# A sink column written by VectorE in place of a one-column product on TensorE, in the banded attention of block 1

## What is computed

```python
def swa_sink_attention(q, k, v, sinks):
    ...
    s = jnp.einsum('bnqhgd,bnkhd->bnhgqk', qb, kk).astype(jnp.float32) * (d ** -0.5)
    ...
    s = jnp.where(mask[None, :, None, None], s, -jnp.inf)
    sink = sinks.astype(jnp.float32).reshape(HKV, G)[None, None, :, :, None, None]
    m = jnp.maximum(jnp.max(s, axis=-1, keepdims=True), sink)
    pexp = jnp.exp(s - m)
    probs = pexp / (jnp.sum(pexp, axis=-1, keepdims=True) + jnp.exp(sink - m))
    o = jnp.einsum('bnhgqk,bnkhd->bnqhgd', probs.astype(v.dtype), vv)
```

## Time and profile before

| | |
|---|---|
| median of 3 runs | 3224.66 us |
| lowest and highest | 3222.48 and 3225.09 us |
| span of the profiled execution | 3222.8 us |
| TensorE busy | 3112.3 us, 97% of the span |
| VectorE busy | 1793.2 us, 56% |
| ScalarE busy | 1251.4 us, 39% |
| mean granted TensorE clock | 0.973 of full speed |

### The profile page before, as it was taken

How to read it: one execution, slowest core, us unless ns; L and a number is a source line. 1 busy time by engine, 2 the same in 40 slices (tenths; PEclk the granted TensorE clock), 3 DMA queues, 4 the chain that set the end, 5 groups by cost and what they waited for, 6 DMA issues and landing times.

```text
span 3222.8 us, 37722 instructions
## 1 busy us (share of the span) xinstructions
PE 3112.3 (97%) x14954; PEld 2462.1 (76%) x14954; DVE 1793.2 (56%) x2509; ACT 1251.4 (39%) x1982; POOL 339.2 (11%) x252
## 2 busy tenths in 40 slices
PE   7999999999999999999998999999999989999998
PEld 5777888887777888886666877888766678778886
DVE  7755643358765544467665735444567657354434
ACT  6644422245644322344444433222334434332222
POOL 2011100011011100011001302000210013020001
PEclk9998999999998999999999999999999999999999
DMA  3111333232111333332112322333211123223332
GB/s 134 53 47 38 94 98 98 93 97 84 54 40 54 94 98 98 94 96 72 53 53 79 118 66 72 98 96 95 84 59 53 46 80 116 66 72 98 98 97 80
DMA packets 73722, 259.09 MB, mean 80 GB/s; under 512 B 8020, under 2 KB 10200, under 8 KB 73176
## 3 DMA queue, kind: packets, MB, share of 16 engines
q1 hardware_dynamic: 72824, 252.99, 24.9%
q0 software_dynamic: 736, 3.87, 0.4%
HBM read 254.73 MB, written 2.10 MB: 80 GB/s over the span
## 4 chain that ended last, share of the span: by engine, by line
PE 87%; DVE 8%; issue 2%; ACT 2%; DVEq 1%; POOLq 0%; DMA 0%; POOL 0%; ACTq 0%
PE bank L479 71%; PE bank L957 2%; DVE w_lo L1934 2%; PE bank L968 1%; PE bank L650 1%; PE bank L978 1%; PE bank L982 1%; PE bank L1153 1%; PE bank L1174 1%; PE bank L994 1%; PE bank L914 1%; PE bank L506 1%; DVE r_x L1969 1%; PE bank L714 1%; ACT w_hi L1276 1%
## 5 line engine op out<-in xcount | busy, mean ns | idle before, releaser
L479 PE MATMUL bank<-a_hi,w_hi 128*128 128x512 f32 x2168 | 880.7, 406 | 37.0 <-DVE w_lo L1934 15.4
L479 PE MATMUL bank<-a_hi,w_lo 128*128 128x512 f32 x2168 | 852.0, 393 | 0.0
L479 PE MATMUL bank<-a_lo,w_hi 128*128 128x512 f32 x2168 | 851.7, 393 | 0.0
L1934 DVE TENSOR_TENSOR w_lo<-w_raw,w_hi 128x1024 fp32r<-128x1024 f32 (+1 forms) x474 | 610.1, 1288 | 288.8 <-ACT w_hi L1276 287.3
L1276 ACT ACTIVATE w_hi<-w_raw 128x1024 fp32r<-128x1024 f32 (+1 forms) x474 | 494.8, 1045 | 441.0 <-DMA w_raw<-weights 439.3
L479 PE MATMUL bank<-b_hi,w_hi 128*128 128x512 f32 (+1 forms) x1560 | 594.6, 381 | 17.2 <-DVE w_lo L1934 9.8
L479 PE MATMUL bank<-b_lo,w_hi 128*128 128x512 f32 (+1 forms) x1560 | 584.0, 374 | 0.0
L479 PE MATMUL bank<-b_hi,w_lo 128*128 128x512 f32 (+1 forms) x1560 | 583.4, 374 | 0.0
L479 PEld LDWEIGHTS bank<-a_hi,w_hi 128*128 128x128 f32 x2168 | 411.8, 190 | 143.9 <-issue 40.0
L479 PEld LDWEIGHTS bank<-a_lo,w_hi 128*128 128x128 f32 x2168 | 412.3, 190 | 90.6 <-issue 8.6
L479 PEld LDWEIGHTS bank<-a_hi,w_lo 128*128 128x128 f32 x2168 | 411.6, 190 | 88.6
(11 more groups left out here) (295 smaller groups left out, 3024.1 us busy)
## 6 DMA issues: line engine op xcount, KB each, us to landing
w_raw<-weights SPq DMA_DIRECT2D x458, 512.0 KB, 3.5
w_raw<-weights SPq DMA_DIRECT2D x16, 384.0 KB, 3.0
x<-x SPq DMA_DIRECT2D x8, 256.0 KB, 7.8
mem<-mem POOLq DMA_DIRECT2D x2, 1024.0 KB, 5.1
out<-x SPq DMA_DIRECT2D x8, 256.0 KB, 2.1
mem<-mem SPq DMA_DIRECT2D x1, 1024.0 KB, 12.7
ple<-ple POOLq DMA_DIRECT2D x2, 512.0 KB, 4.3
o<-c_level SPq DMA_DIRECT2D x1, 512.0 KB
```

The costliest lines, as they stand in the source:

```text
L479: last = mm(bank[unit_bank(u) if at is None else at][:, 0:cols], w[:, u % SLOTS, ks], t[:, k, 0:cols], start=(k == begun and n == 0), stop ...
L1934: tt(w_lo[:, u % SLOTS, w], w_raw[:, u % SLOTS, w], f32(w_hi[:, u % SLOTS, w]), ALU.subtract).then_inc(w_lo_ready, 1)
```

## The change

The sink products are gone. Once, at the start, VectorE writes the negated sinks of both layers into a small tile, `sinks_n` (16 columns). In each turn the fused instruction of VectorE runs over the scores alone (256 or 128 columns) and takes the negated sink of its head, a column of `sinks_n`, as the initial value of its minimum. The column behind the scores, which the exponential still reads, is written by VectorE with a copy (L2181 of the changed kernel) in front of the fused instruction. Where q = 3 no copy is made: the banks are those of q = 1 of the same heads, with the same number of score columns, and the column still stands. The score products now raise `a_scored`.

```diff
@@
+        sinks_n = place("sinks_n", [P, 8 * LAYERS])
@@
                     for e in range(2):
                         mm(bank[score_banks(l, s)[e]][:, 0:ks.stop - ks.start], half_of(y[:, T_SQ + j, qs(q)], e),
-                           half_of(y[:, T_SK, ks], e), start=True, stop=True)
-                    for e in range(2):
-                        nk, sink = ks.stop - ks.start, col("sinks", l, j + 4 * e)
-                        mm(bank[score_banks(l, s)[e]][:, nk:nk + 1], heads_c[0:4, 0:1].broadcast_to([4, P]), sink[0:4],
-                           start=True, stop=True).then_inc(a_scored, 1)
+                           half_of(y[:, T_SK, ks], e), start=True, stop=True).then_inc(a_scored, 1)
@@
                 tt(lb[:, 0:2], vec[:, b + 2:b + 4], vec[:, b:b + 2], ALU.subtract)
+                b = VCOL["sinks"][0]
+                ts(sinks_n[:, :], vec[:, b:b + 8 * LAYERS], -1.0, None, ALU.mult)
@@
                 def window_maxima(s):
-                    n, q = 16 * l + s, s % 4
-                    nk = P * len(tiles_back(q)) + 1
+                    n, j, q = 16 * l + s, s // 4, s % 4
+                    nk = P * len(tiles_back(q))
                     for e in range(2):
                         i = (2 * n + e) % 8
+                        sink = sinks_n[:, 8 * l + j + 4 * e:8 * l + j + 4 * e + 1]
                         dve.wait_ge(a_scored, 2 * n + e + 1)
-                        b = bank[score_banks(l, s)[e]][:, 0:nk]
-                        dve.tensor_tensor_reduce(out=b, in0=b, in1=band if q else band[:, P:], scale=-1.0,
-                                                 scalar=3e38, op0=ALU.add, op1=ALU.min,
+                        b = bank[score_banks(l, s)[e]]
+                        if q != 3:
+                            dve.tensor_copy(b[:, nk:nk + 1], sink)
+                        dve.tensor_tensor_reduce(out=b[:, 0:nk], in0=b[:, 0:nk], in1=band[:, 0:256] if q else band[:, P:256],
+                                                 scale=-1.0, scalar=sink, op0=ALU.add, op1=ALU.min,
                                                  accum_out=stat_n[:, i:i + 1]).then_inc(a_max, 1)
```

More of the change, by code:

```diff
@@ L247, in build @@
         m_col, g_r, neg_b = place("m_col", [P, 16]), place("g_r", [P, 72]), place("neg_b", [P, 4])
-        assert top[0] <= nc.sbuf_usable_end, (top[0], nc.sbuf_usable_end)
         eps, half_pi, ones = der[:, 0:1], der[:, 1:2], der[:, 2:3]
@@ L253, in build @@
         eps_big = der[:, 3:4]
+        sinks_n = place("sinks_n", [P, 8 * LAYERS])
         root_cols = der[:, 58:62]
+        assert top[0] <= nc.sbuf_usable_end, (top[0], nc.sbuf_usable_end)
         def in_a(name, shape, kb, dt=F32):
```

## The result

The change made the kernel faster: 3198.43 us (median of 4 runs, 3190.61 to 3200.91) against 3224.77 us (4 runs, 3222.48 to 3225.09). The ratio is 0.9919, with a 95% interval from 0.9907 to 0.993; that is 26.3 us. The spans of the profiled executions differ by 26.4 us, and the mean granted clock went from 0.973 to 0.978.

A forecast was written before the change was run, and what follows sets the result against it. TensorE was taken as the bound. Sink products of 12.2 us at the low clock and 3.7 us at the high one, less 2.4 us of copies, made 13.5 us off 3224.66: 3211.2 us, range 3202 to 3218 us.

The forecast's parts named there:

- Bound and place: Whole kernel: TensorE is busy 97% of the span, and the two window stages should each end some 7 us sooner.
- The low-clock turn: Turns at 1.2 GHz: 2.20 instead of 3.14 us without sink products; 13 x 0.94 = 12.2 us gained.
- The high-clock turns: 19 turns at 2.4 GHz: seven give 0.53 us each, 3.7 us; VectorE paces the other twelve, which give nothing.
- The copies: 48 one-column VectorE copies at 0.12 us, 20 of them on the path: 2.4 us against the gain.
- The instruction at the start: One added VectorE instruction ahead of its wait for the positions: costs nothing, 0.2 us if the positions came at once.
- Rival 1: Turns 5 to 8 and value products: the low clock ends sooner, about 8 us more gain, 3203 us; chance 0.13.
- Rival 2: High-clock turns: TensorE's waits let the clock fall sooner, ten to twelve turns slow, 3216 to 3219 us; chance 0.14.
- Rivals 3 and 4: Dear copies make VectorE the bound, 3235 us, chance 0.04; low-clock turns give 0.5 instead of 0.94 us, 3220 us, 0.07.

The follow-up runs named there:

- full_sinks: Kernel before with every sink product widened from 4 rows and 1 column to 128 rows and 128 columns, same result: 3202.81 us, ratio 0.9941.
- after_again: The changed kernel run again without an edit, on another chip: 3196.38 us, ratio 0.9915 to the kernel before.
- no_copies: The changed kernel without its 48 VectorE copies, the sink taking no part: 3196.62 us, ratio 0.9925 to the kernel before.
- split_norm: The changed kernel with the norm's sums split into pairs ahead of the transposes of turns 4 to 7: 3194.45 us, ratio 0.992 to the kernel before.
- split_fill: split_norm plus unread products of 128 rows and 512 columns, one ahead of turn 10's transposes and two ahead of turn 11's, each layer: 3190.24 us, ratio 0.9894.
- fill_after: The changed kernel with three unread products of 128 rows and 512 columns ahead of turn 4's transposes in each layer: 3198.7 us, ratio 0.9927.

## Where the prediction was right and which step failed

**Bound and place: right.** TensorE paces the stages before, and the two stages hold the difference (-27.3 us of stage against -26.4 us of span). What lies outside them is 0.9 us longer, less than it varies between executions.

**The low-clock turn: right, its count wrong.** Such a turn lasts 2.20 us as forecast. But the sum took the 13 low-clock groups of before, subtracted 0.94 us from each and left everything else at the length it had. This is the step that failed: "TensorE paces these turns" was taken to mean that the other rows of the turn keep their times. They have their times from the clock, and the clock depends on what is removed. An account by the table: the low-clock sink products, 12.2 us; the high-clock ones, 19 x 0.53 = 10.1 us; other work that no longer runs at 1.2 GHz, 37.6 - 12.2 = 25.4 us that now take half of it, 12.7 us; less 6.2 us of new waits. That is 28.8 us against 27.3 measured. (The rows say rather that work takes 0.55 of its time at the high clock, 1.15 to 0.63 us for scores and 1.05 to 0.59 for transposes; that makes 11.4 instead of 12.7 and 27.5 in all.) The term of 11 to 13 us was in no part of the sum. By place, the low time went down by 6.8 us up to turn 4, which may be chance of these two executions, by some 20.5 us in the middle and by 10.2 us at the end. full_sinks confirms it from the other side: with the products all there and the clock held, 20.5 us are gained.

**The high-clock turns: right in kind, the gain put too small.** VectorE paces them afterwards, and turns 2 to 4 last 1.58 to 1.73 us (1.5 to 1.8 forecast); turns 10 and 11 last 2.43 and 2.87 us, since VectorE's round there is longer than the 1.53 us of one turn. Of the 10.1 us, 6.2 went into waits (those for the copies and those of turns that used to run at the low clock among them), which leaves 3.9; the forecast for that was 3.7 - 2.4 = 1.3. The prediction also took TensorE's share too small: its 1.0 us without the sink products, and "about the same" as 1.53 with them, hold for a turn with scores of 128 columns (0.42 + 0.59, and 0.53). With 256 columns it is 0.63 + 0.59 = 1.22, and 1.75 with them (242.75 to 244.50), so TensorE was the slower one in such turns. The turns that were said to give nothing, less 0.12 us for each copy, gave 0.75 us a layer between the transposes of turn 0 and turn 4; the scalings of turn 4 beside GpSimd have their part in that.

**The copies: right in sign, too dear.** 0.065 us each and not 0.12, so 20 of them make 1.3 us instead of 2.4; the runs can't tell either from nothing. The duration of a row was the wrong measure: the row lasts 0.16 to 0.21 us, yet the next instruction starts 0.065 us behind its start. The Trainium skill's fixed part of about 150 cycles ("VectorE: DVE Perf Modes", section on the TRN2 errata), 0.16 us by the estimate in the prediction, agrees with that duration and not with the distance; by the measurement the distance decides. The initial value from memory costs about 0.04 us for each pass (0.81 us for two passes up to the reciprocal, against 0.73 in the earlier trace rows), inside the bound of 0.1.

**The instruction at the start:** nothing of it is seen, and these runs could not tell 0.2 us.

**Rival 1, which had 0.13, is what happened**, and it was too small. I let the clock come back only one or two turns into turns 5 to 8. It did, behind the transposes of turn 7, the third of them, and the value products of the first layer went from 5.95 to 3.28 us. In the second layer they went from 4.86 to 3.85 us: the 5.95 us that the prediction used for both was the first layer's alone. The prediction's price for this rival was 3203 us, 3200 at the far end. What was missing is the end of the stage, where the low time went from 20.4 to 10.2 us, and the fall at 235 us. The argument against it, that half of the value products had passed before the clock came back, looked at one way back and took its delay for a rule; in the changed kernel the clock came back ahead of them.

**Rival 2 was not the outcome, but it is not nothing.** TensorE waits 0.88 and 0.51 us in turns 1 and 2 and less in 3 and 4. In the profile of the change the clock stays at 1.00 there; in after_again, no_copies, split_norm and split_fill it falls behind these waits in five of their eight layers, each time for 3.4 us. That is far from the ten to twelve turns that the rival asked for. My own argument against it, that "what is taken away streams almost nothing", is the right one, and I used it only to say that the clock wouldn't get worse. Read once more it says that taking such products out leaves the same work in less time, which speaks for a clock that comes back sooner; with seven turns at 0.50 in the first layer alone, that was an argument for rival 1. The Trainium skill ("TensorE: Matmul & The Clock Gate", the section on why this matters for kernels) asks for TensorE to be kept busy, without long gaps. That the fall at turn 11 is gone in both layers of split_fill, where its waits are filled, agrees with it. It does not explain a TensorE that is busy 2.00 of 2.00 us at 0.50: there the kind of product counted, and not the gaps.

**Rivals 3 and 4** fell with the copies at 0.065 us and the low-clock turn at 2.20 us.

**What stays open.** Why the clock comes back in turn 7 and not earlier, and when it falls in the first turns. What the two remedies are worth apart: split_norm alone can't be told from the change by its time, and only both edits together can. Each kernel has one trace, so the low time of a single place is one draw. That the copies are worth nothing was measured at 10 and 4 runs, so to within some 3 us by the narrower of the two.

## What to carry to other kernels

Where a stretch of the profile has a granted clock of 0.50 with TensorE fully busy, look for products of few rows or one column in it: their price here was not only their own time, but up to half the time of what ran at the low clock around them. When products are removed, moved or added there, cost it at both clocks, and work out the sum of the case in which the clock changes over every stretch before giving it a chance. Two remedies helped here: hand such tiny products to another engine, and where TensorE has to wait, fill the wait with full products whose result nobody reads. The second has to fit into the wait: in split_fill it came with the fastest version, in fill_after it gained nothing.

## What the runs showed of the hardware

- The granted clock went with how much of the array the products used, in one profiled execution of each kernel. With 64 products of 4 rows and 1 column the stages spent 61.5 us at 1.2 GHz; with 128 rows and 1 column 58.1; with 4 rows and 128 columns 64.9; with 128 rows and 128 columns 10.3.
- A pair of float32 products of 128 columns and 128 rows takes 0.55 us of TensorE at 2.4 GHz (950.04 to 950.59 in full_sinks) and one of 1 column and 4 rows 0.53 us. The small one saves next to nothing in itself, and in the kernel before it cost 20.5 us against the full one.
- More work can be less time: six full products in all made the kernel before 10 us faster (0.9964 [0.995, 0.9978]).
- A float32 product of 512 columns and 128 rows took 0.85 us at 2.4 GHz: split_fill's two groups of one and of two such products last 1.13 and 1.98 us.
- A one-column copy from SBUF to PSUM on VectorE is listed with 0.16 to 0.21 us and delays the next instruction by 0.065 us; by the source view of after:

```profile
L2181 DVE COPY bank<-sinks_n x48: 153/204/214, 234.2 to 969.8; 128x1 f32<-128x1 f32 x48
...
L2182 DVE CUSTOM_DVE_ANT_0 bank<-bank,small,sinks_n x64: 350/484/494, 234.3 to 971.8; 128x256 f32<-128x256 f32 x48, 128x128 f32<-128x128 f32 x16
```
